# Gate and up projections of a dense SwiGLU as seven quarter-matrix products, with a later table's preparation moved, in a float32 Trainium2 kernel

## What is computed

```python
D_MODEL = 1024
SEQ = 256
CTX_LEN = 256
D_FF = 2816
...
def swiglu(h, w_gate, w_up, w_down):
    return (jax.nn.silu(h @ w_gate) * (h @ w_up)) @ w_down
```

## Time and profile before

| | |
|---|---|
| time, median of 3 runs | 1899.57 us |
| lowest and highest of the 3 | 1899.31 and 1903.55 us |
| the profiled execution's own time | 1903.45 us |
| its span, first to last instruction | 1901.7 us |
| TensorE busy | 1805.2 us, 95% of the span |
| VectorE busy | 475.2 us, 25% |
| ScalarE busy | 353.8 us, 19% |
| mean granted TensorE clock | 0.980 of full |
| HBM read | 389.36 MB, 205 GB/s over the span |

### The profile page before, as it was taken

One profiled execution on the slowest core, in us unless ns is written; L12 is line 12 of the kernel. 1 busy time (PEld: TensorE's weight loads), 2 busy tenths in 40 slices (PEclk: granted clock), 3 DMA queues, 4 the chain that ended last, 5 costly groups with the idle time before them and its releaser, 6 DMA issues.

```text
span 1901.7 us, 21203 instructions
## 1 busy us (share of the span) xinstructions
PE 1805.2 (95%) x8908; PEld 837.1 (44%) x8908; DVE 475.2 (25%) x1108; ACT 353.8 (19%) x765; POOL 41.1 (2%) x87
## 2 busy tenths in 40 slices
PE   6999999899999999999888879999999999999996
PEld 3655454344444444435766754344344422222222
DVE  5978412410002300026584160000000000000002
ACT  3425541210000000014365232000000000000001
POOL 3100000300000000000000000000000000000000
PEclk9999999999999999999999979999999999999998
DMA  9315432542212222343244028999999999999992
GB/s 310 117 23 196 147 102 89 165 123 89 74 59 88 61 61 61 105 165 118 50 157 112 1 114 303 383 372 394 348 372 365 402 365 391 395 408 338 409 389 110
DMA packets 178367, 396.06 MB, mean 208 GB/s; under 512 B 41155, under 2 KB 88491, under 8 KB 172122
## 3 DMA queue, kind: packets, MB, share of 16 engines
q1 hardware_dynamic: 174816, 393.33, 57.4%
q0 software_dynamic: 2192, 1.24, 0.3%
q10 hardware_dynamic: 1258, 0.07, 0.0%
HBM read 389.36 MB, written 1.05 MB: 205 GB/s over the span
## 4 chain that ended last, share of the span: by engine, by line
PE 90%; ACT 4%; DVE 3%; DMA 1%; issue 1%; ACTq 0%; DVEq 0%
PE ps L890 88%; PE ps L893 2%; DMA ring<-in_w_in_dram 1%; DVE rstd L1670 1%; ACT dg L609 1%; DVE work L1687 0%; ACT work L701 0%; ACT work L600 0%; ACT work L601 0%; DVE hT L1692 0%; DVE rstd L1844 0%; ACT work L584 0%; ACT sq L648 0%; ACT aT L714 0%; DVE aT L1846 0%
## 5 line engine op out<-in xcount | busy, mean ns | idle before, releaser
L890 PE MATMUL ps<-ring,work 128*64 128x512 f32 (+4 forms) x2656 | 553.4, 515 | 1.7 <-ACT work L834 1.1
L890 PE MATMUL ps<-aT,ring 128*128 128x512 f32 (+1 forms) x1152 | 454.4, 553 | 7.2 <-ACT work L701 2.7
L890 PEld LDWEIGHTS ps<-ring,work 128*64 128x64 f32 (+2 forms) x2656 | 188.7, 136 | 352.0 <-issue 348.5
L890 PEld LDWEIGHTS ps<-aT,ring 128*128 128x128 f32 x1152 | 219.5, 191 | 233.1 <-issue 218.5
L890 PE MATMUL ps<-work,ring 128*128 128x512 f32 (+1 forms) x480 | 198.3, 571 | 7.3 <-DVE tick L1851 5.9
L1990 DVE TENSOR_TENSOR work<-work,ps 128x512 f32<-128x512 f32 (+4 forms) x26 | 20.1, 779 | 600.2 <-PE ps L890 600.2
L890 PEld LDWEIGHTS ps<-work,ring 128*128 128x128 f32 x480 | 92.2, 192 | 110.9 <-issue 99.6
L890 PE MATMUL ps<-aT,work 128*64 128x512 f32 (+3 forms) x640 | 133.2, 528 | 0.0
L890 PE MATMUL ps<-work 64*64 64x128 f32 (+5 forms) x1664 | 121.4, 275 | 2.4 <-DVE work L1973 1.7
L843 ACT ACTIVATE work<-ps 128x512 f32<-128x512 f32 (+3 forms) x36 | 19.0, 529 | 556.5 <-PE ps L893 556.5
L890 PEld LDWEIGHTS ps<-work 128*64 128x64 f32 (+3 forms) x1664 | 85.3, 152 | 37.6 <-issue 33.8
(11 more groups left out here) (304 smaller groups left out, 1044.8 us busy)
## 6 DMA issues: line engine op xcount, KB each, us to landing
ring<-in_moe_w_down_dram SPq DMA_DIRECT2D x70, 1024.0 KB, 8.4
ring<-in_moe_w_gate_dram SPq DMA_DIRECT2D x50, 1024.0 KB, 7.8
ring<-in_moe_w_up_dram SPq DMA_DIRECT2D x48, 1024.0 KB, 10.3
ring<-in_w_ada_dram SPq DMA_DIRECT2D x23, 2048.0 KB
ring<-in_moe_w_up_dram SPq DMA_DIRECT2D x32, 768.0 KB, 7.9
aT<-in_moe_w_down_dram SPq DMA_DIRECT2D x18, 1024.0 KB, 8.1
ring<-in_moe_w_gate_dram SPq DMA_DIRECT2D x24, 768.0 KB, 6.7
aT<-in_moe_w_up_dram SPq DMA_DIRECT2D x16, 1024.0 KB, 8.1
```

Source lines behind the costliest of these rows:

```text
L890: return pe.matmul(o, lhs, rhs, start=start, stop=stop)
```

## The change

Gate and up are now computed by Strassen's scheme (in Winograd's form). The product of one weight matrix and the tokens is cut in halves three ways: the hidden channels (1408 and 1408), the channels summed over (512 and 512) and the tokens (first and second 128 of each stream, so a half is 256 tokens). In place of eight products of quarters there are seven, of sums of quarters.

- A block b = 2i + j is for gate (j = 0) or up (j = 1) and gives 128 hidden channels of the first half and 128 of the second: 22 blocks in all. TensorE does 7 products of 4 matmuls each, each matmul with 256 tokens, in the order 1, 5, 2, 6, 3, 7, 4, each product in its own bank (0 to 6).
- VectorE makes four sums of weight quarters for each block, one block ahead (`weight_sums`, 512 wide), four sums of token quarters once (`T_of`, 1024 wide), and seven additions for each block that join the products (`combine`, 256 wide). The product of gate and up is made twice for each i, 512 wide, as before 22 in all.
- ScalarE copies products 1 and 5 out of PSUM for each block, and makes `silu` of the joined gate values from SBUF.
- A load ("ffn", i) has four transfers of 512 KB, with rows of 128 floats, in place of two with rows of 256. A load's slot is freed by its 14th product.
- The sums lie where tables of layer 1 lay (`Sums` 0 to 4096, `Tsum` 15872 to 18944). So `load_b(1)`, `load_c(1)` and `out_table(1, 0)` move into the down projection (behind its copies m = 2 and m = 3), `turn_c(1)` behind its m = 2 on TensorE, and the 8 transfers of SyncE and 32 of GpSimd start when the last product is done.
- Semaphores of both layers are merged into one where they were two (`centred`, `ln_used`, `glu_used` and others), with counts to match. No order changes by that.

The diff, without those renamed semaphores:

```diff
+        FU = FN // 2
+        FH = KC // 2
+        Sums = view(0, [2, 4, FH, P], "j s k m")
+        Tsum = view(15872, [3, FH, 2, P], "n k i t")
+        by_half = lambda v: v.rearrange("p (i h t) -> p i h t", i=2, h=2)
+        B_of = aT[:].rearrange("p k (i h t) -> p k i h t", i=2, h=2)
+        def T_of(n):
+            return B_of[:, 0:FH, :, 1, :] if n == 3 else Tsum[:, {1: 0, 2: 1, 4: 2}[n]]
+        PRODUCTS = (1, 5, 2, 6, 3, 7, 4)
+        def product(n):
+            return ps[:, PRODUCTS.index(n), 0:256].rearrange("p (i t) -> p i t", i=2)
+        def carried(b, n):
+            return sq[:, b % 2, 256 * n:256 * n + 256].rearrange("p (i t) -> p i t", i=2)
...
-                    steps.append([cols(ffn_gate[0], 256 * i, 256 * i + 256), cols(ffn_up[0], 256 * i, 256 * i + 256, 2048)])
-                    used.append(("ffn_done", 2 * i + 2))
+                    steps.append([cols(w, FF // 2 * h + P * i, FF // 2 * h + P * i + P, 2048 * j + 1024 * h)
+                                  for j, w in enumerate((ffn_gate[0], ffn_up[0])) for h in range(2)])
+                    used.append(("ffn_p", 14 * i + 14))
...
-                if n == at["ffn", 3]:
-                    sp.wait_ge(sem("y_done1"), KC)
+                if n == at["down"] + 2:
+                    sp.wait_ge(sem("ffn_p"), 14 * FU)
                     load_b(1)
...
             load_c(0)
-            pool.wait_ge(sem("y_done1"), KC)
+            pool.wait_ge(sem("ffn_p"), 14 * FU)
             load_c(1)
...
+                    for b in range(2 * FU):
+                        if b >= 2:
+                            act.wait_ge(sem("ffn_c"), 7 * b - 7)
+                        for i, n in enumerate((1, 5)):
+                            act.wait_ge(sem("ffn_p"), made(b, n))
+                            act.activation(carried(b, i), product(n), ACT.Copy).then_inc(sem("ffn_t"), 1)
+                        if b % 2 == 0:
+                            for i, n in enumerate((4, 7)):
+                                act.wait_ge(sem("ffn_c"), 7 * b + n)
+                                act.activation(sg[:, i, :], sg[:, i, :], ACT.Silu).then_inc(sem("ffn_silu"), 1)
...
+            def strassen_in():
+                def make(b, n, lhs, rhs):
+                    if b == 0 and n >= 4:
+                        pe.wait_ge(sem("ffn_tokens"), {5: 1, 6: 2, 7: 3, 4: 4}[n])
+                    if b:
+                        taken = {2: 1, 6: 2, 3: 3, 7: 5, 4: 7}
+                        pe.wait_ge(*(sem("ffn_c"), 7 * b - 7 + taken[n]) if n in taken else
+                                   (sem("ffn_t"), 2 * b - 2 + (1, 5).index(n) + 1))
+                    for k in range(FH):
+                        if b == 0 and n <= 2:
+                            pe.wait_ge(sem("a_ready2"), 2 * (k if n == 1 else FH + k) + 2)
+                        last = mm(product(n), lhs(k), rhs(k), k == 0, k == FH - 1)
+                    last.then_inc(sem("ffn_p"), 1)
+                for b in range(2 * FU):
+                    i, j = b // 2, b % 2
+                    if j == 0:
+                        step_in(at["ffn", i])
+                    a1, a2 = weights(at["ffn", i], 2 * j), weights(at["ffn", i], 2 * j + 1)
+                    s1, s2, s3, s4 = [Sums[:, j, n] for n in range(4)]
+                    make(b, 1, lambda k: a1[:, k, :], lambda k: B_of[:, k, :, 0, :])
+                    pe.wait_ge(sem("ffn_s"), 4 * b + 1)
+                    make(b, 5, lambda k: s1[:, k, :], lambda k: T_of(1)[:, k])
...
-                        if i == 12:
-                            pe.wait_ge(sem("mod"), 4)
-                            turn_c(1)
+                    strassen_in()
+                    def tables():
+                        pe.wait_ge(sem("mod"), 4)
+                        turn_c(1)
                     pe.wait_ge(sem("hid_ready"), FN)
-                    project(3, at["down"], P, lambda k: hid[:, k, :], lambda k: None, FN, ALL)
+                    project(3, at["down"], P, lambda k: hid[:, k, :], lambda k: None, FN, ALL, tables)
...
+                    def weight_sums(b):
+                        n, j = at["ffn", b // 2], b % 2
+                        if j == 0:
+                            dve.wait_ge(sem(f"ring_in{n % 3}"), landed[n])
+                        if b >= 2:
+                            dve.wait_ge(sem("ffn_p"), made(b - 2, 7))
...
+                        tt_(o[0], a21, a22, ALU.add).then_inc(sem("ffn_s"), 1)
+                        tt_(o[2], a11, a21, ALU.subtract).then_inc(sem("ffn_s"), 1)
+                        dve.wait_ge(sem("ffn_s"), 4 * b + 1)
+                        tt_(o[1], o[0], a11, ALU.subtract).then_inc(sem("ffn_s"), 1)
+                        dve.wait_ge(sem("ffn_s"), 4 * b + 3)
+                        tt_(o[3], a12, o[1], ALU.subtract).then_inc(sem("ffn_s"), 1)
...
+                    weight_sums(0)
+                    dve.wait_ge(sem("a_ready2"), 2 * KC)
...
+                    tt_(T_of(1), first[1], first[0], ALU.subtract).then_inc(sem("ffn_tokens"), 1)
...
+                        combine(b, c11, product(2), sum1, product_of=2)
+                        combine(b, sum1, product(6), sum1, after=1, product_of=6)
+                        combine(b, c12, product(3), p5, product_of=3)
+                        combine(b, c12, c12, sum1, after=3)
+                        combine(b, sum1, product(7), sum1, after=4, product_of=7)
...
+                        combine(b, c22, p5, sum1, after=5)
+                        combine(b, c21, product(4), sum1, product_of=4)
+                        if j:
+                            dve.wait_ge(sem("ffn_silu"), 2 * i + 2)
+                            dve.wait_ge(sem("ffn_c"), 7 * b + 7)
+                            tt_(second, second, sg[:, 1, :], ALU.mult).then_inc(sem("hid_ready"), 1)
```

More of the change, by code:

```diff
@@ L1033, in project @@
                     last.then_inc(sem(f"y_done{n}"), 1)
+                    if between and m == 2:
+                        between()
             for l in range(L):
@@ L1053, in turn_u @@
                     if i < 4:
-                        pe.wait_ge(sem(f"t1_copied{l}"), 4)
+                        pe.wait_ge(sem("t1_copied"), 4 * l + 4)
                     else:
@@ L1695, in add_back, with copy_y @@
                 tt_(hT[:, KC - 1, cs], hT[:, KC - 1, cs], y(KC - 1, cs), ALU.add).then_inc(sem(f"h_ready{n}"), 1)
-            def copy_y(n, y):
+            def copy_y(n, y, between=None):
                 for m in range(KC):
@@ L1700, in copy_y @@
                     dve.tensor_copy(y(m, norm_cols(n)), ps[:, m % 4, norm_cols(n)]).then_inc(sem(f"y_copied{n}"), 1)
+                    if between:
+                        between(m)
             def recur(l, h, within=None, after=None):
@@ new lines, in combine @@
+                    def combine(b, out, a, of, after=0, product_of=None):
+                        if product_of:
+                            dve.wait_ge(sem("ffn_p"), made(b, product_of))
+                        if after:
+                            dve.wait_ge(sem("ffn_c"), 7 * b + after)
+                        tt_(out, a, of, ALU.add).then_inc(sem("ffn_c"), 1)
+                    weight_sums(0)
+                    dve.wait_ge(sem("a_ready2"), 2 * KC)
+                    first, second = [[B_of[:, FH * j:FH * j + FH, :, h, :] for h in range(2)] for j in range(2)]
@@ new lines, in _ @@
+                    tt_(T_of(1), first[1], first[0], ALU.subtract).then_inc(sem("ffn_tokens"), 1)
+                    dve.wait_ge(sem("ffn_tokens"), 1)
+                    tt_(T_of(2), second[1], T_of(1), ALU.subtract).then_inc(sem("ffn_tokens"), 1)
+                    tt_(T_of(3), second[1], first[1], ALU.subtract).then_inc(sem("ffn_tokens"), 1)
+                    dve.wait_ge(sem("ffn_tokens"), 2)
+                    tt_(T_of(4), second[0], T_of(2), ALU.subtract).then_inc(sem("ffn_tokens"), 1)
@@ new lines, in _ @@
+                    for b in range(2 * FU):
+                        i, j = b // 2, b % 2
+                        if b + 1 < 2 * FU:
+                            weight_sums(b + 1)
+                        if b == 4:
+                            modulate(1, 0, 7, rowsT)
+                        if i and j == 0:
+                            dve.wait_ge(sem("hid_ready"), 2 * i)
+                        first, second = (hid[:, i, :], hid[:, FU + i, :]) if j else (sg[:, 0, :], sg[:, 1, :])
+                        c11, c12 = [by_half(first)[:, :, h] for h in range(2)]
+                        c21, c22 = [by_half(second)[:, :, h] for h in range(2)]
+                        sum1, p5 = carried(b, 0), carried(b, 1)
+                        dve.wait_ge(sem("ffn_t"), 2 * b + 2)
+                        combine(b, c11, product(2), sum1, product_of=2)
[4 more added lines that the diff above has]
+                        if j:
+                            dve.wait_ge(sem("ffn_silu"), 2 * i + 1)
```

(7 more changed lines are left out.)

78 lines of the change are left out of this document (34 added, 44 removed).

## The result

| | before | changed |
|---|---|---|
| time, median | 1901.56 us (4 runs, 1899.31 to 1904.24) | 1875.12 us (4 runs, 1874.75 to 1875.46) |
| ratio, 95% interval | | 0.986 [0.9843, 0.9877] |
| span of the profiled execution | 1901.7 us | 1872.9 us |
| mean granted clock | 0.980 | 0.979 |

The change makes the kernel 26.4 us faster by the medians (1901.56 - 1875.12). The four runs of the kernel before fall in two groups, two near 1899.4 and two near 1903.9, so that their median is a time that none of them had, while the changed kernel's four lie within 0.7 us. The forecast was 1872, in a range of 1865 to 1883: right in sign and in mechanism.

A forecast was written before the change was run, and what follows sets the result against it. TensorE alone was taken to bound gate and up. Product 5 at 388.7, plus 10.3, 253.5, 1.7, 1.2 and 0.9 us, gave 656.3 against 684.45: 28.2 us less, so 1872 us, range 1865 to 1883.

The forecast's parts named there:

- The matmuls: Gate and up on TensorE: 616 matmuls of 256 tokens replace 352 of 512, 265.6 us for 302.1, -36.5 us.
- The start: Block 0: product 5 waits for weight sums and the first token sum until 388.7; TensorE idles 6.2 us.
- The clock: Behind TensorE's wait before product 5: low granted clock adds 1.7 us, bounds 0 and 3.4.
- The end: From gate and up's last matmul to the down projection: an addition and a multiplication, 1.2 us where 1.4 passed before.
- The tables: Layer 1 tables moved into the down projection: eight transposes, 0.87 us, change stage, neutral in total; the rest hides.
- The loads: Gate and up weight loads: 2 MB in 7 us instead of about 6, in time for use, costed at nothing.
- VectorE: Steady blocks of gate and up: VectorE busy 6.6 us of 12.07, 55%, so TensorE's waits are met early.
- A price at each border: Weight loads exposed at each of 154 product borders: 29 us (1901) or, with matmul run-out, 55 us (1926); chance 5%.
- The clock falls again and again: Steady gate and up: one low clock stretch in each block costs 36 us, giving 1908; chance 2%.
- VectorE the bound: Steady blocks: VectorE needs 13.2 us, twice its sum; stage 25 us longer, 1896, about no change; chance 2%.
- A heavier start: Block 0: clock low twice as long and token sums at 1.67 us, giving 1875; inside the forecast, no separate chance.

The follow-up runs named there:

- the kernel kept at work: Changed kernel with 15 useless matmuls of 256 tokens added in block 0, beside product 1 and between it and product 5; 1872.50 us.
- the combined kernel: Changed kernel with block 0's weight sums before the norm's reciprocal, product 2 ahead of product 5, first token sum awaiting only its own 8 shifts; 1868.06 us.

## Why the prediction was right, and by how much it was off

On a common axis (the first changed trace moved by the 0.76 us that it was early), the forecast had the down projection start at 655.4 ahead of the moved transposes, and it started at 657.2. Term by term:

- **The matmuls.** 12.07 a block was forecast, 12.09 measured: +0.3 us over 21 blocks. The kernel with product 4 cut short showed that this term is the whole block. The half-long matmuls cost half, the weight loads fit beside them, and 616 replace 352: this is where the gain comes from.
- **The start.** Product 5 was forecast at 388.7 and came at 388.46 on that axis: the sum of tokens took 1.22 us, as reckoned from two shorter ones. The idle time was 5.09 instead of 6.2 us, mostly because product 1, with the clock already low, ended at 383.4 on that axis and not at 382.5. That did not change when product 5 starts.
- **The clock: the term that was mis-sized.** The forecast added 1.7 us within bounds of 0 and 3.4; the changed trace gives 13.49 - 48 x 0.2158 = 3.1 (0.2158 us is the beat of a record), against the kernel kept at work it is 3.05, and the second execution of the changed kernel gives 12.22 - 10.36 = 1.9. The prediction took one wait of 3.66 us as the model, with a short low stretch behind it. Here the low level began before the idle time, in product 1, and lasted through the idle time, product 5 and product 2 (into product 6 in the first execution). This is +1.4 of the 1.8 us in the first execution and +0.2 in the second: the size of this term varies from one execution to the next, within the stated bounds.
- **The end:** 1.3 us instead of 1.2, and a last matmul that ran out 0.16 after the beat.
- **The tables:** neutral, as forecast; the kernel with them alone shows it, and the idle time behind `out_table` agrees to 0.1 us.
- **The loads:** nothing, as forecast. From 392 to 394 us no transfer is on its way (DMA share 0.00), and the first sum from the second load starts at 401.73 without a wait.
- **VectorE:** 6.1 us a block instead of 6.6 (51% for 55%). Instructions that don't wait for each other start sooner than their records are long: the sums of 512 at 0.60 us intervals, with records of 0.69.

That leaves 26.3 us of gain for 28.2 (27.6 in the second execution). The forecast of the time was 1899.57 - 28.2 = 1871.4, said as 1872. The 3.7 us from 1871.4 to 1875.12 are 1.8 of gain and 2.0 of baseline: the kernel before had a median of 1901.56 in the comparison. The prediction's other figure, 1875.3 from the profiled execution, is near the measured time partly by luck: in that pair of executions 1.8 us too much of forecast gain were made up by 0.76 us ahead of the stage and 1.7 behind it.

**The rivals.** *A price at each border:* refuted. In 238 us TensorE shows no idle time, and the product shortened to one matmul kept all borders and gave its full saving in each block. *The clock falls again and again:* refuted for this stage. The granted clock is 1.00 over 238 us with seven products in turn through the banks; it fell once, at the start. The Trainium skill (TensorE: Matmul & The Clock Gate, "A second HAM failure mode: psum-queue depth-cycling") tells of a bf16 kernel that cycled through banks, in which TensorE idled shortly between groups of matmuls so often that the clock went down and up. Here the banks cycle too, and the trace shows neither: no idle time in 238 us, and a clock of 1.00. With the sums made four times TensorE did wait between groups, and the clock fell behind three waits of 2.60 us and not behind those of up to 1.30. *VectorE the bound:* refuted at this size by the doubled sums, shown at the quadruple. *A heavier start:* in the first execution it was this rival's clock loss, nearly at its bound, with the sum of tokens as forecast.

## What to carry to other kernels

When one engine does all the work, an algorithm that takes an eighth of it away gives that eighth, provided that the added work of the others fits in the beat; here VectorE had room from 51% up to over 73% of a block. What is lost is at the edge: look for the first product that needs something newly made, put the ones that need nothing ahead of it, and make its inputs in the idle time of the stage before. Price a wait on TensorE together with the clock behind it, by what the engine does ahead of the wait as well.

## What the hardware showed that was not expected

- TensorE's clock fell while the engine was at work: in the changed kernel at 380.2 us, 1.2 us into product 1, whose matmuls came at the pace of ScalarE's shifts behind an idle time of 2.21 us. It stayed at 0.50 until 393.9, with 5.09 us idle in between; in a second execution of the same kernel it fell at 381.9 and rose at 392.1. In the combined kernel, without that idle time, it was low from 380.9 to 384.3 alone. The kernel before had the same idle time and the same pace of shifts, with matmuls of 512 tokens, and kept 1.00. There a matmul (0.858 us) outlasts the two shifts that it waits for (6.50 / 8 = 0.81 us), so TensorE had no pause; one of 256 tokens (0.432 us) does not. That this decides is not shown (timeline of TensorE and a window of it):

```profile
379.79 6.67 PE L890 MATMUL ps<-aT,ring 128*128 128x512 f32 x15 [2.21 <-ACT aT L662]
```

```profile
380.00:382.00 2.00, 2.00 (x5) 0.81 (x5) 2.00 (x6) 2.00 (x7) 0.00 (x0) 1.00 1.11 357
```

- The length of an idle time alone does not tell whether the clock falls: it fell to 0.50 behind 2.60 us in the kernel with the sums made four times, and stayed at 1.00 behind 2.21 us in the kernel before and behind 1.30.
- Useless matmuls kept it at 1.00 in one kernel (2.21 us idle ahead of them, then 38 records in 8.44 us) and not in the other (3.15 us idle ahead, 32 records in 8.83 us). The two differ in more than one thing, so what decides between them stays open.
